# Starts of the branch outputs, merged branches and feed-forward activations in SBUF moved by 32, 64 and 96 bytes

## What is computed (the reference, cut)

```
h = rmsnorm(x, g_mix);  proj = h @ w_in          # q k v, forget, lru x/gate, memory q, gate logits
y_fox, y_lru, y_mem = ...                        # three branches, (256, 1024) each
y_d    = einsum('bsnc,ncd->bsnd', stack(y_fox, y_lru, y_mem), w_branch)
gates  = sigmoid(gate_logits + b_gate)
x = x + sum(gates * y_d, axis=2) @ w_out
up = causal_depthwise_conv(rmsnorm(x, g_ffn) @ w_ffn_up, w_ffn_conv, b_ffn_conv)
u_act, u_val = split(up, 2)
return x + (gelu(u_act) * u_val) @ w_ffn_down    # hidden width 5632
```

## Time and profile before

| | |
|---|---|
| device time, median of 3 runs | 1649.64 us (1647.93 to 1649.79) |
| span of the profiled execution, first to last instruction | 1645.8 us |
| TensorE busy | 1632.6 us (99%), 9008 matmuls |
| VectorE, ScalarE, GpSimd busy | 65%, 53%, 2% |
| granted TensorE clock, mean | 0.998 |
| HBM read | 304.69 MB, 186 GB/s over the span |

### The profile page before, as it was taken

One profiled execution on the slowest core, in us unless ns is written; L12 is line 12 of the kernel. 1 busy time (PEld: TensorE's weight loads), 2 busy tenths in 40 slices (PEclk: granted clock), 3 DMA queues, 4 the chain that ended last, 5 costly groups with the idle time before them and its releaser, 6 DMA issues.

```text
span 1645.8 us, 26208 instructions
## 1 busy us (share of the span) xinstructions
PE 1632.6 (99%) x9008; PEld 1411.6 (86%) x9008; DVE 1064.5 (65%) x1277; ACT 879.0 (53%) x1200; POOL 38.6 (2%) x41
## 2 busy tenths in 40 slices
PE   9999999999999999999999999999999999999998
PEld 7778888788888888888888888888888888888887
DVE  6855578755656565564766777777777777544443
ACT  7656667456554444554555655555555555434332
POOL 0000111000000000000011000000000000000000
PEclk9999999999999999999999999999999999999999
DMA  8554456655455555555555555555565565655653
GB/s 346 179 166 151 144 173 194 209 181 164 154 186 187 190 181 196 186 189 191 180 191 191 179 190 179 192 195 186 180 202 174 184 204 189 198 195 191 204 196 103
DMA packets 85260, 307.42 MB, mean 187 GB/s; under 512 B 9880, under 2 KB 10656, under 8 KB 85088
## 3 DMA queue, kind: packets, MB, share of 16 engines
q1 hardware_dynamic: 83952, 302.88, 55.0%
q0 software_dynamic: 1120, 3.94, 0.8%
q10 hardware_dynamic: 144, 0.01, 0.0%
HBM read 304.69 MB, written 2.11 MB: 186 GB/s over the span
## 4 chain that ended last, share of the span: by engine, by line
PE 98%; DVE 1%; ACT 0%; DMA 0%; issue 0%; ACTq 0%; DVEq 0%
PE psG L345 95%; PE psM L345 2%; PE psM L430 0%; DMA par_sb<-par 0%; DVE normed L1019 0%; DVE W L981 0%; ACT W L621 0%; DVE X L1165 0%; PE psM L466 0%; DVE x_n L1261 0%; ACT fox_square L650 0%; PE psM L464 0%; DVE sq_x L1209 0%; DVE sq_x L1207 0%; DVE mem_v L986 0%
## 5 line engine op out<-in xcount | busy, mean ns | idle before, releaser
L981 DVE TENSOR_TENSOR W<-raw,W 128x1024 fp32r<-128x1024 f32 x566 | 687.0, 1226 | 359.0 <-ACT W L621 358.4
L345 PE MATMUL psG<-X,W 128*128 128x512 f32 (+1 forms) x4864 | 853.0, 337 | 0.0
L345 PEld LDWEIGHTS psG<-X,W 128*128 128x128 f32 x4864 | 741.6, 188 | 108.3
L621 ACT ACTIVATE W<-raw 128x1024 fp32r<-128x1024 f32 x566 | 590.6, 1055 | 365.1 <-PE psG L345 354.4
L345 PE MATMUL psG<-hidden,W 128*128 128x512 f32 (+1 forms) x1408 | 245.4, 337 | 0.0
L345 PEld LDWEIGHTS psG<-hidden,W 128*128 128x128 f32 x1408 | 214.0, 188 | 31.3
L345 PE MATMUL psG<-W,X 128*128 128x512 f32 x768 | 179.8, 394 | 0.0
L629 ACT ACTIVATE low<-psG 128x512 f32<-128x512 f32 x116 | 69.4, 598 | 188.7 <-PE psG L345 188.7
L345 PEld LDWEIGHTS psG<-W,X 128*128 128x128 f32 x768 | 144.4, 189 | 29.8
L345 PE MATMUL psG<-Y,W 128*128 x768 | 134.4, 337 | 0.0
L345 PEld LDWEIGHTS psG<-Y,W 128*128 128x128 f32 x768 | 117.0, 188 | 17.1
(11 more groups left out here) (184 smaller groups left out, 560.7 us busy)
## 6 DMA issues: line engine op xcount, KB each, us to landing
raw<-w_units SPq DMA_DIRECT2D x566, 512.0 KB, 3.4
xs<-xT SPq DMA_DIRECT2D x4, 512.0 KB, 8.1
outT<-xs POOLq DMA_DIRECT2D x7, 256.0 KB, 3.5
mem_raw<-first_data SPq DMA_DIRECT2D x3, 512.0 KB, 5.0
mem_raw<-memT SPq DMA_DIRECT2D x3, 512.0 KB, 7.4
lru_rg<-w_rg POOLq DMA_DIRECT2D x8, 128.0 KB, 3.8
c_all<-c_rows POOLq DMA_DIRECT2D x1, 1024.0 KB, 8.3
outT<-xs SPq DMA_DIRECT2D x2, 128.0 KB, 1.8
```

The lines of the kernel that those rows point to most:

```text
L345: return nc.tensor.matmul(*a, skip_group_check=True, **kw)
L621: nc.scalar.activation(W[:, s, :, 0], raw[:, s], ACT.Copy).then_inc(hi_done, 1)
L981: V.tensor_tensor(W[:, s, :, 1], raw[:, s], f32(W[:, s, :, 0]), ALU.subtract).then_inc(lo_done, 1)
```

## The change

```diff
-        Y = sb("Y", [P, 3, BT, 2, T], 96 * KB, F32R)
-        M0, G_0, T0 = 144 * KB, 176 * KB, 192 * KB
+        Y = sb("Y", [P, 3, BT, 2, T], 96 * KB + 32, F32R)
+        M0, G_0, T0 = 144 * KB + 64, 176 * KB + 64, 192 * KB + 64
...
-        rstd2 = sb("rstd2", [P, T], T0 + 5 * KB)
-
-        hidden = sb("hidden", [P, FT, 2, T], 96 * KB, F32R)
-        up_pad = {w: sb(f"up_pad{w}", [P, 2, 2 + T], 184 * KB + w * 2080) for w in range(2)}
-        up_c = {w: sb(f"up_c{w}", [P, 2, T], 184 * KB + 4160 + w * 2048) for w in range(2)}
-        low = sb("low", [P, 2, 2, T], T0 + 6 * KB)
+        rstd2 = sb("rstd2", [P, T], T0 + 4 * KB)
+
+        hidden = sb("hidden", [P, FT, 2, T], 96 * KB + 96, F32R)
+        up_pad = {w: sb(f"up_pad{w}", [P, 2, 2 + T], 184 * KB + 96 + w * 2080) for w in range(2)}
+        up_c = {w: sb(f"up_c{w}", [P, 2, T], 184 * KB + 96 + 4160 + w * 2048) for w in range(2)}
+        low = sb("low", [P, 2, 2, T], 198 * KB)
```

## The result

The changed kernel takes 1653.36 us (median of 14 runs, 1649.24 to 1654.33) against 1648.16 us (14 runs, 1646.66 to 1649.79): a ratio of 1.0029 with a 95% interval of 1.0021 to 1.0036. It is slower by 0.29%, where I had forecast no change. The profiled execution has a span of 1651.9 us against 1645.8, 6.1 us more.

The account below looks back on a forecast made before the run. TensorE's matmul pace was taken to bound the kernel. All terms summed to 0, leaving the span at 1645.8 us and the timed median at 1649.6 us (1651.2 with the moving operands' near end); range 1646 to 1657 us.

Parts of the forecast that it names:

- What bounds the kernel: Whole kernel: TensorE's pace decides, with 98% of the chain and no waits from 458.65 to 1641.11 us; VectorE and ScalarE have slack.
- Moving operands: 2688 matmuls moving Y, merged and hidden: 0 from their new starts, judged by lru_xr; near end 0.6 ns each, 1.6 us.
- Relative starts: Moving against stationary starts of matmuls, XM's 384 in the memory phase included: neither gain nor loss, 0, judged by ff_w.
- the ff_w row: Evidence: float32r matmuls with stationary starts at 0, 32, 64, 96 in turn, read as 226.7 ns gaps against 227.3 ns unstaggered.
- Regions and neighbours: SBUF regions and other engines' accesses: no effect on TensorE, so a better spread against them has nothing to win.
- VectorE and ScalarE: Their instructions on moved tiles: 0, with a bound of 3.0 us on the taps, under VectorE's 359.0 us of idle.
- Transfers: DMA: raw and par_sb stay, lru_rg and ff_raw arrive 64 bytes further on off the chain; nothing new waits.
- The slower one: Y and hidden matmuls: an off-line start costs one more line, 6.7 ns each, 14.5 us, 1664.1 us; chance 0.11 in any form.
- The mark that I had named for it: Sign of the slower rival: window of down at 254.7 us in place of 245.3, with up unchanged at 478.6.
- The faster one: Moved-operand matmuls: the 14 ns are a weight-load and moving-read clash that staggering removes, up to 38.2 us, 1611.5 us; chance 0.06.
- The 0.83 for "same": Whole kernel: chance 0.83 that the time stays 1649.6 us, within 0.2%.

Follow-up runs that it names:

- the last experiments: 40 stationary columns instead of 128 in the first quarter's gates, with X, Y, merged, hidden at distance 96, 0 or 64 from W: 1666.74, 1648.91, 1640.29 us.
- all at 64: Against the changed kernel, XM back at its old start and Y, merged, hidden all 64 bytes past a multiple of 128: 1643.51 us, ratio 0.9973.

## Why the prediction was wrong

**What bounds the kernel** was right: TensorE, without waits from 460 us on, so that each ns per matmul is in the time. That made a change of 1% per matmul visible at all.

**Moving operands** failed first: the term that I had put at 0 measured -0.6 us on Y, -0.8 on merged and +3.5 on hidden. My nearest row was lru_xr, moving at 32 against mem_PT at 0. But its stationary operand lru_rg starts at 32 as well, so both rows have distance 0, and my own sentence said so. The row bore on the own start, which is what doesn't matter, and said nothing of the distance, which does. Nor would a distance have shown in it: lru_xr is plain float32, and mem_PT, also plain float32, kept its 216 ns at a distance of 64. Y measured -0.8 ns per matmul, merged -1.7 and hidden +2.5, where I had taken 0 with an end of +0.6.

**Relative starts** failed for another reason. I did look at the distance there, and took the ff_w row for its proof. It had three faults: the stationary operand has 40 columns and not 128, which the last experiments show to change the price; the distances (eight by the period of 256 bytes) follow one another from matmul to matmul, so that no steady pace arises; and starts given to 0.1 us leave an error of some 6.7 ns in the mean of 15 gaps (0.1/15 us). Read to the nanosecond from the same trace, the starts are 230.7 ns apart on average, from 224 to 235, and not 226.7: 4 ns over the wide matmuls at distance 0. So the row did show a cost, of the distances or of its shape. What I called a proof was a misread row with another shape. The sentence that XM falls under the same row cost +6.7 ns x 384 = 2.6 us of the 3.96 lost there; for the clock the prediction had no term.

**Regions and neighbours** held. Y, merged and hidden have one and the same unit at the same distance, and the share of work on VectorE and ScalarE plays no part. **VectorE and ScalarE** held: the medians of their forms on the moved tiles kept their durations to 4 ns, with 359 us of cover turned into 367. **Transfers** held.

**The rivals.** The slower one had the sign but not the mechanism: it charged a start off a line, while hidden pays by its distance and merged at 64 gains. It asked for 9.4 us in down, and 3.5 came. The mark that I had named for it, a longer down beside an unchanged up, is there. The faster one named the right pair, the two reads of TensorE, and a stagger does win: 4.5 us of its 38.2 with all at 64. But it held every stagger for a gain, while 96 costs 40 ns a unit and any stagger costs the wide phases. The Trainium skill's "SBUF — State Buffer", section "Who interferes with whom", lists two read ports for TensorE, one for the moving operand and one for the weight load, and calls them independent. The trace agrees that no other engine gets in the way: up and down have the same unit of 2787 ns before, with VectorE busy 76% and 48% of them. It doesn't agree that the two are indifferent to each other's addresses: units of 2760 to 2827 ns by the distance alone.

The measured time lay inside my range, the 0.29% outside what I called the same. That it lay inside owes something to luck: the range had been widened upwards for another mechanism, and gains of 1.4 us on Y and merged offset part of the losses. The 0.83 for "same" stood on two rows of which neither had the distance and the shape of the work in question. The honest price of an unseen distance would have been a range on both sides of zero with less than half the chance in the middle.

## What to carry to other kernels

In a float32r kernel that TensorE bounds, the start addresses of the two operands of a matmul are a parameter worth 0.5%: measure the distance between them modulo 256 bytes for each shape, since one layout won 1% a matmul in the narrow phases (64 bytes) and lost 3% in the wide ones. When a row of a trace is to stand for a case it doesn't show, write down every property of both operands first; a neighbour that shares the looked-at property but also shares the hidden one proves nothing. Read gaps from the starts themselves and not from rounded first and last starts. Compare start-to-start times over a stage, which here are mostly steady to 2 ns in thousands, before times of whole runs, which here scatter by 0.1%.

## What the runs showed of the hardware that was not expected

- A stream of float32r matmuls runs in a fixed cycle, whose length depends on the distance of its two operands modulo 256 bytes: 2760 to 2827 ns for a unit of 6144 columns, at a granted clock of 1.00. Plain float32 matmuls show nothing of it (215.6 ns a matmul at 0, 215.8 at 64). Where the units of a narrow stage are constant they lie 13.3 ns apart: 2760, 2773, 2787, 2800, 2813, 2827. At 224 (2802 to 2816), and in the wide phases at 96 (2805 to 2815), they vary within the stage.
- At a distance of 96 bytes there are two such cycles, 2827 and 2800 ns a unit, and at 160 two as well, 2813 and 2827. Which one a stage falls into differs between kernels with the same addresses, and at 160 between the quarters of one kernel; in up at 96 it stayed for all 171 units and on through down.
- The clock has its own share in the scatter of the runs. The lowest of the 14 runs of the changed kernel (1649.24 us) is the only one with a mean granted clock of 1.000; the others have 0.998 or 0.999. Two stretches of 3.4 us at half the clock cost at most 3.4 us, an estimate from the trace, and 3.4 us off the median are 1649.96. So the clock alone comes near that run; it wasn't profiled.
- With 40 stationary columns in place of 128 a matmul isn't faster, and at distances of 0 and 64 it is slower by 1.7 and 4.2 ns. Why is open, as is the mechanism behind the distance.
